# Output projections in split column halves, with the feed-forward's first inputs prepared between them

## The reference

```
# first block
x = x + recurrent_block(x)        # ... (gelu(y) * rg_lru(conv(...))) @ a_w_out
x = x + swiglu(rmsnorm(x)*g)      # hidden 2816
x = x + nsa_layer(x)              # 16 heads, three softmaxes, gates ... o @ b_w_out
x = x + swiglu(rmsnorm(x)*g)
# second block
x = x + hybrid_mixer(rms_norm(x)) # gated linear attention + stick breaking ... y @ w_out
x = x + swiglu_2(rms_norm(x))     # hidden 3584
x = x + hybrid_mixer(rms_norm(x)) # ... y @ w_out
x = x + moe_swiglu(rms_norm(x))   # 8 experts, top 2 of 8
return rms_norm(x)
```

## Time and profile before

| | |
|---|---|
| median of 3 runs | 2581.16 us |
| the profiled execution's own time | 2593.58 us |
| its span, first to last instruction | 2592.0 us |
| TensorE busy | 2433.8 us, 94% |
| VectorE busy | 1652.1 us, 64% |
| ScalarE busy | 1338.6 us, 52% |
| mean DMA rate | 227 GB/s over the span, about 360 GB/s in the mixture of experts |
| mean granted TensorE clock | 0.979 of 2.4 GHz |

### The profile page before, as it was taken

One profiled execution on the slowest core, in us unless ns is written; L12 is line 12 of the kernel. 1 busy time (PEld: TensorE's weight loads), 2 busy tenths in 40 slices (PEclk: granted clock), 3 DMA queues, 4 the chain that ended last, 5 costly groups with the idle time before them and its releaser, 6 DMA issues.

```text
span 2592.0 us, 30679 instructions
## 1 busy us (share of the span) xinstructions
PE 2433.8 (94%) x12234; PEld 1975.8 (76%) x12234; DVE 1652.1 (64%) x1472; ACT 1338.6 (52%) x1184; POOL 58.6 (2%) x68
## 2 busy tenths in 40 slices
PE   7899998998998999899989988999999999999998
PEld 6488845767888896788789866777777877778876
DVE  5255535526546654555575557788878888888877
ACT  3244303425435663433457525666666667666765
POOL 0000010000000000000000001000000000000010
PEclk9999998999999999999999999999999999999999
DMA  6275363006553323555333237999999999999995
GB/s 217 82 259 194 132 229 114 1 17 240 180 182 106 131 98 130 195 194 194 138 130 130 98 138 286 348 358 357 356 345 357 368 363 362 368 354 374 369 375 213
DMA packets 251090, 588.53 MB, mean 227 GB/s; under 512 B 6476, under 2 KB 14864, under 8 KB 251008
## 3 DMA queue, kind: packets, MB, share of 16 engines
q1 hardware_dynamic: 244160, 564.27, 59.8%
q0 software_dynamic: 6656, 23.04, 2.4%
q10 hardware_dynamic: 192, 0.05, 0.0%
HBM read 573.19 MB, written 14.16 MB: 227 GB/s over the span
## 4 chain that ended last, share of the span: by engine, by line
PE 60%; DMA 16%; DVE 12%; ACT 9%; issue 2%; SPq 0%; ACTq 0%; DVEq 0%; PEldq 0%
DMA raw<-in_moe_w_gate 13%; PE ps L583 10%; PE ps L585 10%; PE ps L584 10%; DVE wl L1638 7%; PE ps L539 7%; ACT wh L1191 7%; PE ps L892 3%; PE ps L894 3%; PE ps L893 3%; DMA raw<-in_moe_w_down 2%; PE ps L531 2%; PE ps L838 1%; PE ps L794 1%; PE ps L779 1%
## 5 line engine op out<-in xcount | busy, mean ns | idle before, releaser
L1638 DVE TENSOR_TENSOR wl<-raw,wh 128x4096 fp32r<-128x4096 f32 (+1 forms) x221 | 968.9, 4386 | 246.6 <-ACT wh L1191 246.2
L1191 ACT ACTIVATE wh<-raw 128x4096 fp32r<-128x4096 f32 (+1 forms) x221 | 796.1, 3603 | 471.5 <-PE ps L585 187.5
L583 PE MATMUL ps<-wh,xmh 128*128 128x512 f32 x896 | 360.5, 402 | 34.2 <-DVE wl L1638 13.4
L584 PE MATMUL ps<-wl,xmh 128*128 128x512 f32 x896 | 352.7, 394 | 0.0
L585 PE MATMUL ps<-wh,xml 128*128 128x512 f32 x896 | 352.6, 394 | 0.0
L583 PE MATMUL ps<-wh,hh 128*128 128x512 f32 x712 | 279.5, 393 | 13.4 <-DVE hl L1653 13.3
L585 PE MATMUL ps<-wh,hl 128*128 128x512 f32 x712 | 278.0, 390 | 0.0
L584 PE MATMUL ps<-wl,hh 128*128 128x512 f32 x712 | 277.8, 390 | 0.0
L583 PE MATMUL ps<-wh,xh 128*128 128x512 f32 (+1 forms) x632 | 247.3, 391 | 17.5 <-issue 14.3
L584 PE MATMUL ps<-wl,xh 128*128 128x512 f32 (+1 forms) x632 | 243.1, 385 | 0.0
L585 PE MATMUL ps<-wh,xl 128*128 128x512 f32 (+1 forms) x632 | 243.1, 385 | 0.0
(11 more groups left out here) (477 smaller groups left out, 3378.4 us busy)
## 6 DMA issues: line engine op xcount, KB each, us to landing
raw<-in_moe_w_gate SPq DMA_DIRECT2D x56, 2048.0 KB, 9.7
raw<-in_moe_w_up SPq DMA_DIRECT2D x56, 2048.0 KB, 9.6
raw<-in_moe_w_down SPq DMA_DIRECT2D x56, 2048.0 KB, 9.5
raw<-in_w_in SPq DMA_DIRECT2D x22, 2048.0 KB, 8.0
raw<-in_f_w_in SPq DMA_DIRECT2D x20, 2048.0 KB, 8.4
raw<-in_f_w_out SPq DMA_DIRECT2D x10, 2048.0 KB, 8.1
raw<-in_dense_w_gate SPq DMA_DIRECT2D x7, 2048.0 KB, 7.7
raw<-in_dense_w_up SPq DMA_DIRECT2D x7, 2048.0 KB, 8.2
```

What stands on the lines that cost most here:

```text
L583: mm(ps[:, bank, 0:n], xa, a, start=(begin and k == 0), stop=False)
L584: mm(ps[:, bank, 0:n], xa, l, start=False, stop=False)
L1191: fn(wh[:, kind, 0:n], raw[:, s, 0:n], ACT.Copy).then_inc(wh_full[kind], 1)
L1638: v.tensor_tensor(wl[:, kind, 0:n], raw[:, plan[name][kind][0], 0:n], wh[:, kind, 0:n].bitcast(F32), ALU.subtract).then_inc(wl_full[kind], 1)
```

## The change

It moves or rewrites code at all four sites; what follows is the diff in its core.

- One helper for all sites, `out_project`: four column halves of 256, weights split (`high_out`, `low_out`), 48 matmuls each (`natural`), one addition to x for both token tiles (`add_columns`), PSUM ring g = banks 3, 4, 5.
- The inputs of sites 0 and 1 are split as well: `uh`, `ul`. At site 0 the multiplication by `yg` is cut in two, then ScalarE copies and VectorE subtracts, in two pieces each. At site 1 `outputs` becomes a copy, a wait for it and a subtraction.
- The first two halves of site 0's weights are split on ScalarE between the gelu pieces and on VectorE behind the scan; those of site 1 inside the attention loop (ScalarE after steps 15 and 17, VectorE in steps 16 and 18).
- At sites 0 to 2 the barrier and `norm(split="raw")` go. Finished columns of x are turned behind the next half (`turn_columns`) and split (`high_columns`, `low_columns`); the first gate weights are split after the second half has been used up, the first up weights later. The first token tile of the feed-forward starts with the columns that are there (`first_tile`).
- `wmo` and `ul` get places of their own under the other stages' tensors, and tensors of stages one and two are moved to make room. Two DMAs of GpSimd wait for other semaphores than the barriers'.

```diff
+            def turn_columns(site, q):                                   # TensorE
+                pe.wait_ge(x_added, 4 * site + q + 1)
+                b = me.s.claim(pe)
...
+            def out_project(site):
+                for q in range(4):
+                    me.see(mh_ready)
+                    me.see(ml_ready)
+                    b = me.g.claim(pe)
+                    natural(b, wmo[:, q % 2], out_view(site, q, raw_low)).then_inc(x_filled, 1)
+                    out_used[site, q] = (x_filled, me.g.n)
+                    if q % 2:
+                        released(out_key(site, q), me.g)
+                    if q and SITES[site][1]:
+                        turn_columns(site, q - 1)
-            me.see(yh_ready)
-            for t in range(2):
-                arrived(pe, ("a_out", t))
-                for m in range(M):
-                    product(me.v, ("a_out", t), m, rg)
-                released(("a_out", t), me.v)
             drained(me.v)
+            drained(me.a)
+            me.see(ul_ready, 2)
+            out_project(0)
...
-                norm(split="raw")
+                def first_tile():
...
+                    filled(0)
+                    pe.wait_ge(s_read, me.s.n - 1)
+                    first_product(0, U0, w0, range(0, 4))
+                    turn_columns(site, 3)
+                    split_columns(2)
+                    first_product(0, U0, w0, range(4, 6))
+                    if w0 < FB:
+                        filled(1)
+                        first_product(1, U0, w0, range(0, 6))
+                    split_columns(3)
+                    first_product(0, U0, w0, range(6, KD)).then_inc(g_done, 1)
+                    if w0 == FB:
+                        filled(1)
+                    first_product(1, U0, w0, range(6 if w0 < FB else 0, KD)).then_inc(u_done, 1)
...
+            def out_project(site):                                       # ScalarE
+                high_out(site, 2)
...
+                high(name, 0, 0, U0, KD * w0)
+                high_columns(site)
+                high_out(site, 3)
+                high_columns(site)
+                high(name, 1, 0, U0, KD * w0)
+                high_columns(site)
+                high_columns(site)
...
+                if f in (3, 5):
+                    high_out(0, f // 2 - 1)
...
+            for j in range(2):
+                me.see(yh_ready)
+                fn(uh[:, 4 * j:4 * j + 4, :], rg[:, 4 * j:4 * j + 4, :], ACT.Copy).then_inc(uh_ready, 1)
...
+                if i in (15, 17):
+                    high_out(1, (i - 15) // 2)
...
+            def out_project(site):                                       # VectorE
+                add_columns(0)
+                low_out(site, 2)
...
+                low(name, 0, B0, n0)
+                low_columns(site)
+                add_columns(1)
+                low_out(site, 3)
+                low_columns(site)
+                add_columns(2)
+                if w0 < FB:
+                    low(name, 1, B0, n0)
+                add_columns(3)
+                low_columns(site)
+                low_columns(site)
+                if w0 == FB:
+                    low(name, 1, B0, n0)
...
+            low_out(0, 0)
+            low_out(0, 1)
             me.see(yg_ready)
-            v.tensor_tensor(rg[:], rg[:], yg[:], ALU.mult).then_inc(yh_ready, 1)
+            for p_ in parts:
+                v.tensor_tensor(rg[:, p_, :], rg[:, p_, :], yg[:, p_, :], ALU.mult).then_inc(yh_ready, 1)
+            for p_ in parts:
+                me.see(uh_ready)
+                v.tensor_tensor(ul[:, p_, :], rg[:, p_, :], uh[:, p_, :].bitcast(F32), ALU.subtract).then_inc(ul_ready, 1)
...
-                    v.tensor_copy(oT[:, h // 2, m * P:(m + 1) * P], ps[:, b, 0:P]).then_inc(o_read, 1)
+                    link(v.tensor_copy(uh[:, h // 2, o], ps[:, b, 0:P]))
+                    v.tensor_tensor(ul[:, h // 2, o], ps[:, b, 0:P], uh[:, h // 2, o].bitcast(F32),
+                                    ALU.subtract).then_inc(o_read, 1)
...
+                if i in (16, 18):
+                    low_out(1, i // 2 - 8)
```

More of the change, by code:

```diff
@@ L813, in _ @@
             me.scores_end()
[L814 to L821, removed]
+            drained(me.a)
+            drained(me.o)
+            out_project(1)
             ffn("ffn1", (me.s, me.s))
@@ L887, in half_natural @@
                     wh_, wl_ = parts(q)
[L888 to L895, removed]
+                    natural(ring.claim(pe), wh_, wl_).then_inc(ring.filled, 1)
                     half_used[layer, q] = (ring.filled, ring.n)
@@ L1009, in mixer @@
                 drained(me.s)
[L1010 to L1013, removed]
                 drained(me.v)
+                out_project(2 + layer)
             mixer(0)
-            me.barrier("ffn2")
             ffn("ffn2", (me.s, me.s))
             mixer(1)
+            pe.wait_ge(x_added, me.g.n)
             me.barrier("moe")
@@ L1564, in residual, with low_out, add_columns @@
[L1564 to L1568 removed]
+            def low_out(site, q):
+                me.see(mh_ready)
+                v.tensor_tensor(out_view(site, q, raw_low), out_view(site, q), wmo[:, q % 2].bitcast(F32),
+                                ALU.subtract).then_inc(ml_ready, 1)
+            def add_columns(q):
+                b = me.g.take(dve)
+                xs = x[:, :, q * HW:(q + 1) * HW]
+                v.tensor_tensor(xs, xs, ps[:, b, :].rearrange("p (m n) -> p m n", m=M), ALU.add).then_inc(x_added, 1)
@@ new lines, in low_columns @@
+            def low_columns(site):
+                _, _, g, off = SITES[site]
+                j = me.turned % 4
+                me.turned += 1
+                b = me.s.take(dve)
+                me.see(norm_h)
+                for kk_ in range(2):
+                    k = 2 * j + kk_
+                    t = v.scalar_tensor_tensor(xl[:, k, :], ps[:, b, kk_ * S:(kk_ + 1) * S], col(g, off + k),
+                                               xh[:, k, :].bitcast(F32), ALU.mult, ALU.subtract)
+                t.then_inc(s_read, 1)
@@ L2104, in mixer @@
                 low_sum(1)
-                for q in range(4):
-                    b = me.v.take(dve)
-                    xs = x[:, :, q * HW:(q + 1) * HW]
-                    v.tensor_tensor(xs, xs, ps[:, b, :].rearrange("p (m n) -> p m n", m=M), ALU.add).then_inc(v_read, 1)
-                    if q < 2:
-                        low_half(Q_OUT + 2 + q)
             mixer(0)
-            me.barrier("ffn2")
-            ffn("ffn2", "ffn_norm_2", 0, beside=lambda: low_tile(1))
+            ffn(2, beside=lambda: low_tile(1))
             mixer(1)
+            out_project(3)
             me.barrier("moe")
```

211 lines of the change are left out of this document (118 added, 93 removed).

## The result

| | before | after |
|---|---|---|
| median | 2582.9 us (6 runs) | 2561.3 us (6 runs) |
| ratio to the runs beside it | | 0.991 (0.988 to 0.993) |
| the same kernel once more | 2587.4 (12 runs; 1.002, 0.9996 to 1.004) | 2572.1 (6 runs; 0.995, 0.994 to 0.997) |
| profiled execution, span | 2592.0 us | 2548.8 us |

One of the first six runs of after took 7051.85 us; it is left out of the ratio, and the median of the other five is 2559.3. The kernel is faster by 0.9% in the first measurement and by 0.5% in the second. So there are two questions: where the 43.2 us between the two spans come from, and why two measurements of one kernel differ by 11 us.

A forecast was written before the change was run, and what follows sets the result against it. TensorE, busy for 94% of the span, was taken as the bound, with time to come from its idle places or cheaper matmuls. 3.9 + 1.1 + 4.3 = 9.3 us off 2581.2 gave 2572, range 2563 to 2583.

The forecast's parts named there:

- a difference of the runs and not of the work: Base of the forecast: the runs' median lies 12.4 us below the profiled execution, so the gain was taken off 2581.2.
- One turn at 1.1: Projections of sites 0 to 2: one turn of 8 transposes takes 1.1 us on TensorE, at most 1.5.
- Site 0, 3.9 gained: Site 0: start at 94.0, 1.4 us for the clock, second token tile 35.4 later, at 130.8 against 134.67.
- Site 1, 1.1 gained: Site 1: projection and first tile gain 8.0 us, attention ahead of them gets 6.9 us longer.
- The queue argument: Attention: in VectorE's queue, subtractions delay diagonals (2.2 us, last output 0.3) and two low parts stall TensorE about 2.2 each.
- the clock eats part: Rival: new TensorE gaps cost up to 1.7 us each at half clock; 4 us gained, 2577; chance 0.25.
- attention hides its share: Rival: subtractions and low parts fall into VectorE's idling, the 6.9 us come back; 16 gained, 2565; chance 0.2.
- Site 2, 4.3 gained: Site 2: up products end 4.9 us earlier, less 0.6 for the clock behind a gap of 3 us.
- 3 us ahead of the up products: Site 2: TensorE stands from 1050.1 to 1053.1, waiting for the up weights' low part.
- with 0.2 to spare: Site 2: the last half's low part is done at +13.9, half 3 may start at +13.7; at most 0.5 us lost.
- the slower rival: Rival: halves wait for low parts, 6 us late at site 2, 3.5 at sites 0 and 1; 2590; chance 0.1.
- Site 3 and elsewhere, nothing: Site 3 and the rest: same instructions in the same order, barrier stays, moved tensors change no instruction's shape; 0 us.

The follow-up runs named there:

- the late experts: The changed kernel with 34 plain products of 0.43 us ahead of the barrier before the mixture of experts: 2578.1 us, ratio 0.999.
- the doubled turns: The changed kernel with attention's low parts cut in pieces, its outputs copied without the subtraction, and each turn of site 0 done twice: 2549.5 us in one run.
- the filled ones: The changed kernel with 36 transposes of the identity on TensorE ahead of each of attention's two waits of 2.02 us: 2565.8 us in one run.
- the combined kernel: The changed kernel with attention's low parts in pieces, eleven products ahead of site 0, squares moved earlier, site 2's low parts reordered and cut: 2551.5 us, ratio 0.988.
- the spread: The changed kernel with attention's two low parts on VectorE cut in four pieces each, one per odd step from 17 to 31: 2550.9 us, ratio 0.987.

## Why the prediction was wrong, by its steps

**What the number holds.** The forecast took 9.3 us off the median; the medians moved by 21.6 in the first measurement. The two pairs of traces give 13.7 and 16.4 ahead of the experts, 4.4 to 7.1 more than 9.3: that is the sum's own error, and the terms below are answerable for it. The rest of the 10.7 by which 2572.0 missed 2561.3 is the difference between two measurements of one kernel, whose cause stays open. The forecast left the experts at nothing, and the late experts bear that out. But the step "a difference of the runs and not of the work" put no width on the runs: the range of 2563 to 2583 was made from the sum's unknown costs alone, and the three runs of before (6.6 us apart) couldn't show how far measurements differ.

**One turn at 1.1.** This is the step of the sum that failed: a mis-sized term, in an overlap that worked as described. It counted 8 transposes by 0.12 and a wait. A turn of one column half is 2 column tiles by 2 token tiles, 4 transposes; the row says 0.35, the doubled turns 0.43. The kernel before has four steps of 4 as well, and not of 8 as my description of it says: a row with x8 on its page is two steps merged. Four turns at three sites, some 0.7 us too much each: 8 us. It is in the marks: second tile at site 1 32.5 us behind the start, forecast 35.4. There the last turn starts at 25.5 in place of 27.7, and from its end on the forecast of ScalarE's chain holds. Without this error the sum would have said 17 to 18, and attention's mis-sized term below would have brought it down to 12.

**Site 0, 3.9 gained**: 5.7. The start came at 93.66 for 94.0, the second tile at 128.87 for 130.8. Two errors against each other: turns 2.8 too dear, the clock 1.4 and not the 2.7 that 6.8 us at half clock cost. In the repetition the half clock lasted 3.4 us only, and the tile came at 127.52.

**Site 1, 1.1 gained**: 2.1 lost (the lead falls from 5.7 to 3.6; 0.6 of it ahead of attention's first stall). The projection and first tile gained 10.9 for 8.0, which is the turns. But attention, forecast 6.9 longer, was 12.4. The queue argument held part by part: both stalls at 2.02 for 2.2, the subtraction at 2.5 with 0.5 behind the last output, for 2.2 and 0.3. Missing was the clock: 5.0 behind the two stalls (4.2 by the filled ones) and 1.5 at attention's end (from the last wait for diagonals to the projection after takes 6.6 us, 3.4 of them at half clock, and the combined kernel 5.1, at the full clock), less the 1.1 that after is spared at attention's start. With the stalls' 4.0 these make the 12.4. I had written this as the rival "the clock eats part", two of its gaps were these, and had put 0 into the sum for them. The rival that attention hides its share was shown possible by another order, not by this one: VectorE's 1.4 us of idling holds pieces of 0.69, not a piece of 2.28.

**Site 2, 4.3 gained**: 6.2. The forecast of "3 us ahead of the up products" was 2.76. The fit "with 0.2 to spare" did not hold: the last half came 1.49 late, which is the slower rival's mechanism at a quarter of the 6 us that it named. The turns paid for it, with luck beside them: at this site's start before is at half clock for 3.4 us in both of its traces and after in neither, some 1.6 us that no term of the sum has.

**Site 3 and elsewhere, nothing**: 3.9 us. The same instructions did not keep their price. In each mixer, ahead of its projection, after gains 0.8 us with the same products at the full clock: the matmuls of 256 columns follow each other at 0.118 us and not at 0.120 (45 of them take 5.40 us in before, 940.47 to 945.87, and 5.30 in after, 936.14 to 941.44). The same stretch of the first mixer in before and its repetition, then in after and its repetition:

```profile
872.88:977.34 104.46, 103.58 (x777) 94.61 (x777) 58.26 (x79) 67.98 (x85) 0.00 (x0) 1.00 0.29 102
```

```profile
872.45:976.90 104.45, 103.57 (x777) 94.60 (x777) 58.24 (x79) 67.96 (x85) 0.00 (x0) 1.00 0.29 102
```

```profile
868.99:972.65 103.66, 102.67 (x776) 93.70 (x777) 58.38 (x79) 67.93 (x85) 0.00 (x0) 1.00 0.29 103
```

```profile
865.84:969.49 103.65, 102.67 (x776) 93.69 (x776) 58.40 (x79) 67.92 (x85) 0.00 (x0) 1.00 0.30 103
```

As far as the diff shows, only the tensors' places differ there; that this is the cause is not shown. Another 1.9 came at site 3, most of it from a stretch of 3.4 us at half clock that before has at its start and after has not. With 5.7 at site 0, 2.1 lost at site 1, 1.1 between sites 1 and 2, 6.2 at site 2 and 0.9 behind it this makes the 13.7.

The Trainium skill's rule against idle gaps between matmul bursts ("TensorE: Matmul & The Clock Gate", "Why this matters for your kernels") was the one that I had weighed down at site 0. There the rows side with it: the gap of 5.42 us was followed by half clock in each trace that has it, and by 1.00 where eleven products filled it. Attention's stalls of 2.02 us are shorter than the gaps of which the page's row speaks, and the clock fell behind them all the same.

## What to carry to other kernels

When a long instruction is put into a queue that feeds a busy engine at every step, price what it delays and the clock behind the stall, and cut it to the idle time that the queue shows in each step; here that was worth 9 us. Count the instructions of a helper from its loops before multiplying by a row, as a row may hold several calls of it. Before a range is written, look at how far the unchanged stretches differ between executions, and one measurement of the same kernel from the next: here the experts' stretch, with its queues busy for 0.96 to 0.99, moved by 19 us, and the median by 11.

## What the runs showed of the hardware that I had not expected

The same gap doesn't always cost the same. Behind the 5.42 us ahead of site 0 TensorE was at half clock for 6.8 us in after and for 3.4 in its repetition, whose clock is full from 97 on:

```profile
97.00:100.00 3.00, 3.00 (x28) 3.00 (x27) 0.00 (x0) 0.00 (x0) 0.00 (x0) 1.00 0.02 5
```

Of the seven traces that have this gap, two show 6.8 us and five 3.4. Behind gaps of 1.51 and 1.64 us at the start of site 2 it fell for 3.4 us in the kernel before, for 6.8 in the spread and the combined one, and not at all in after. Here the repetitions of before and of after agree with their first traces, so this is not chance alone; what decides is not shown. At site 0 a stretch of 6.8 us cost 2.7. So an edit that saves 3 us can be given back elsewhere without any wait that shows it, as at site 3 of the combined kernel.

Back to back, a product of 256 columns cost 0.120 us in the kernel before and 0.118 in after, in two traces each. Plain transposes of 128 columns of the identity cost 0.11 in a row of 36, and four of x 0.35 with the step to the next product.
